# Two dense blocks and a mixture of experts on one core: in a mixed pair of expert steps, the overflow blocks' weight loads are listed before the first four's

## The reference

```python
def hierarchical_moe(h, router_group, router_expert, w_gate, w_up, w_down):
    ...
    # 4 groups of 8 experts: the best group, and in it the two best experts of each token
    combine = jnp.sum(jax.nn.one_hot(expert_id, N_EXPERTS, dtype=jnp.float32) * top_w[..., None], axis=1)
    for grp in range(N_GROUPS):
        hg = jnp.einsum("td,edf->tef", ht, w_gate[sl])      # 1024 -> 256 for each of 32 experts
        hu = jnp.einsum("td,edf->tef", ht, w_up[sl])
        act = jax.nn.silu(hg) * hu * combine[:, sl, None]
        y = y + jnp.einsum("tef,efd->td", act, w_down[sl])  # 256 -> 1024
```

## Time and profile before

| | us |
|---|---|
| median of three runs | 2850.46 |
| lowest and highest | 2848.6, 2853.78 |
| the profiled execution | 2856.73 |
| its span, first to last instruction | 2854.6 |
| granted TensorE clock, mean | 0.962 |

### The profile page before, as it was taken

The page is one execution under the profiler, slowest core; times in us unless marked ns, Lnnn a source line. Parts: engine busy times, 40 slices in busy tenths (PEclk is TensorE's granted clock), DMA queues, the critical chain, the costliest instruction groups (busy, mean ns, idle before and its releaser), DMA issues.

```text
span 2854.6 us, 35316 instructions
## 1 busy us (share of the span) xinstructions
PE 2707.4 (95%) x14474; PEld 2163.0 (76%) x14474; DVE 1534.1 (54%) x2709; ACT 968.1 (34%) x1723; POOL 57.5 (2%) x59
## 2 busy tenths in 40 slices
PE   6999999999999999999999989999999989997896
PEld 3888887876667888888888878798998787784343
DVE  3776754356224777738767444645555764444111
ACT  3322224257123322224222243634444533322111
POOL 0000000000000000000000000000000000001320
PEclk8999998999999999999999999999999899997898
DMA  7344442210222444433466423044534122256997
GB/s 300 140 191 181 184 174 75 90 41 1 88 104 98 167 184 183 179 118 148 164 256 266 154 103 111 23 167 148 187 150 167 59 85 73 80 230 254 404 368 300
DMA packets 56959, 456.54 MB, mean 160 GB/s; under 512 B 10720, under 2 KB 21344, under 8 KB 21856
## 3 DMA queue, kind: packets, MB, share of 16 engines
q1 hardware_dynamic: 49600, 446.01, 40.7%
q0 software_dynamic: 6912, 6.32, 0.7%
q10 hardware_dynamic: 288, 1.97, 0.2%
HBM read 497.25 MB, written 1.05 MB: 175 GB/s over the span
## 4 chain that ended last, share of the span: by engine, by line
PE 86%; DVE 5%; DMA 5%; ACT 3%; issue 1%; POOL 0%; SPq 0%; DVEq 0%; ACTq 0%; POOLq 0%
PE ps L497 59%; PE ps L1221 3%; PE ps L1562 2%; PE ps L2173 2%; PE ps L1213 1%; PE ps L3144 1%; DMA wr<-edn 1%; PE ps L1141 1%; PE ps L1118 1%; DMA wr<-eup 1%; DMA wr<-eup,extra_ids 1%; PE ps L502 1%; PE ps L2780 1%; PE ps L2232 1%; DMA BIG<-eup 1%
## 5 line engine op out<-in xcount | busy, mean ns | idle before, releaser
L497 PE MATMUL ps<-UL,fh 128*128 128x512 f32 (+1 forms) x1408 | 517.2, 367 | 22.5 <-DVE UL L751 21.5
L497 PE MATMUL ps<-UH,fl 128*128 128x512 f32 (+1 forms) x1408 | 515.2, 366 | 0.0
L497 PE MATMUL ps<-UH,fh 128*128 128x512 f32 (+1 forms) x1408 | 514.6, 366 | 0.0
L491 DVE TENSOR_TENSOR fl<-wr,fh 128x1024 fp32r<-128x1024 f32 (+1 forms) x304 | 328.7, 1081 | 245.5 <-ACT fh L484 245.4
L484 ACT CAST fh<-wr 128x1024 fp32r<-128x1024 f32 (+1 forms) x304 | 282.7, 934 | 199.2 <-PE ps L497 181.5
L497 PEld LDWEIGHTS ps<-UL,fh 128*128 128x128 f32 x1408 | 268.7, 191 | 68.5 <-DVE UL L751 21.3
L543 DVE SCALAR_TENSOR_TENSOR acc<-wr,CA 128x1024 f32<-128x1024 f32 x256 | 312.7, 1222 | 3.7
L497 PEld LDWEIGHTS ps<-UH,fh 128*128 128x128 f32 x1408 | 269.2, 191 | 42.1
L497 PEld LDWEIGHTS ps<-UH,fl 128*128 128x128 f32 x1408 | 269.3, 191 | 41.5
L497 PE MATMUL ps<-HH,fh 128*128 128x512 f32 (+1 forms) x704 | 255.2, 363 | 0.0
L497 PE MATMUL ps<-HL,fh 128*128 128x512 f32 (+1 forms) x704 | 255.2, 362 | 0.0
(11 more groups left out here) (501 smaller groups left out, 4178.0 us busy)
## 6 DMA issues: line engine op xcount, KB each, us to landing
wr<-ws SPq DMA_DIRECT2D x130, 2048.0 KB, 7.8
wr<-ws SPq DMA_DIRECT2D x32, 1408.0 KB, 5.9
BIG<-eup SPq DMA_DIRECT2D x30, 1024.0 KB, 19.7
wr<-eup SPq DMA_DIRECT2D x28, 1024.0 KB, 12.3
BIG<-edn SPq DMA_DIRECT2D x15, 1024.0 KB, 18.4
wr<-edn SPq DMA_DIRECT2D x14, 1024.0 KB, 15.4
wr<-ws SPq DMA_DIRECT2D x8, 1536.0 KB, 6.4
wr<-ws SPq DMA_DIRECT2D x9, 1024.0 KB, 4.8
```

What stands on the lines that cost most here:

```text
L491: e.tensor_tensor(lv, raw_tile(sp.units[n]), hv.bitcast(F32), ALU.subtract).then_inc(*low_done.inc("low", event))
L497: i = e.matmul(out, l, r, start=first and n == 0, stop=last and n == len(pairs) - 1, skip_group_check=True)
```

## The change

`expert_loads()` lists a pair's loads with its two fours the other way round whenever one of them is a beyond four. The list is used for handing out places and for the order on the two issuing queues. The order of TensorE's steps, `QUADS` and everything else stay.

```diff
@@ -214,9 +214,12 @@
 def expert_loads():
 
+
     out = []
     for g in range(FOURS // 2):
         quads = (2 * g, 2 * g + 1)
+        if "beyond" in (QUADS[p][0] for p in quads):
+            quads = quads[::-1]
         out += [("eup", n, h) for h in range(2) for p in quads for n in slots_of(p)]
         out += [("edn", n, 0) for p in quads for n in slots_of(p)]
     return out
```

## The result

Six runs of the changed kernel have a median of 2864.8 us (2858.43 to 2870.8), six runs of the kernel before beside them 2852.89 us (2848.6 to 2854.93). The ratio is 1.0039, 95% interval 1.0029 to 1.005: **slower by about 11.1 us** (8.3 to 14.3), where 6.7 had been forecast. 2864.8 lies above the range's upper end of 2861.

The account below looks back on a forecast made before the run. The prediction asked whether and when the DMA engines run dry, since the experts end when the last weights land. Its terms 5.8 + 0.4 + 0.5 = +6.7 us on 2850.46 gave 2857.2 us, range 2852.5 to 2861.

Parts of the forecast that it names:

- the last seam: Pair 4 to 5: eight loads start only at 2775.86 at the earliest, DMA engines run dry, +5.8 us (4.9 to 6.5).
- the first seam: Pair 0 to 1: beyond 0's up loads come earlier, first 2's later; forecast as +0.4 and +0.5 us.
- Rival C: Last seam: its eight loads find the DMA engines still busy, order among equal loads worth 0, 2850.5 us; chance 0.06.
- the step from the rule to "worth 0": All queues share the same 16 DMA engines, so moving loads between queues' turns is worth 0; time stays 2850.5 us.
- up a0 of pair 1: First seam: this up step starts at 2647.3 instead of 2642.44, +4.8 us, as beyond loads share the time.
- together +0.5: Pair 1's down a: real down loads 1.2 us earlier, a 2.9 us wait, 1.7 us slower step; bounds -2.5 and +2.
- The 0.4 us without work: Pair 1's down loads wait for the later up a0: moving restarts at 2655.4 against 2655.0, +0.4 us dry.
- It carries a shift of pair 1 on about one to one.: Chain from pair 1's down b through pairs 2 to 4, to the issue at 2775.86, passes on pair 1's shift.
- rival B: Pair 1's down b ends 2.5 us earlier, pair 2's up b1 stops waiting, gaps fill: +2.3 us, 2852.8; chance 0.20.
- Between two mixed pairs nothing changes: Pairs 2, 3 and 4: old and new order hand over places in the same way, so no time is added.
- X itself covers them, 0: First seam: SyncE's issue behind X is held until X moves, now holding three loads; cost 0.
- rival D: Later up a0 of pair 1 opens a gap of some 3 us, nothing returns it: +9.7 us, 2860.2; chance 0.13.

Follow-up runs that it names:

- the kernel that has this seam alone: Kernel before, with pair 5's places handed to first 7's four before first 6's, issue order kept: 2861.05 us, 1.0029.
- the first seam alone: Changed kernel with pair 5's places handed out in the other order and X's load issued third of its four: 2854.29 us, 1.0006 against the kernel before.

## Why the prediction was wrong in size

**Right: the last seam.** Predicted: no issue until up b1 of pair 4, five in a row, eup 24,0 landing 6.0 us after its issue, the end +5.8 (4.9 to 6.5). After: issued at 2778.89, landed 5.4 us later; 6.0 us dry; +6.2 in the ledger, +6.5 in the kernel that has this seam alone. Its size by itself is less sure: 8.3 us by the ratio in the order of before, 3.4 between the two kernels with the first seam and X third (1.0018 and 1.0006), where the hole is 4.1 us since up b1 of pair 4 was not slow. Rival C and the step from the rule to "worth 0" fall: 1.0029 for other places with the same order of issue, 1.0021 for another order with the same places. That the queues share one total rate is not touched by this.

**Right: up a0 of pair 1.** +5.1 against 4.8, a wait of 9.01; up a1 without its 5 us wait.

**Too small: pair 1.** The term "together +0.5" was 3.0. Its down loads did not land 1.2 us earlier (4.33 us of wait instead of the 2.9 of the sum), and the matmuls after the wait took 6.08 us, 2.4 more than 3.64, not 1.7. The 0.4 us without work ahead of it doesn't show: no window from 2604 to 2680 is under 0.96 busy.

**Wrong: "It carries a shift of pair 1 on about one to one."** +3.0 became -1.5 in pair 2, since up a1 no longer waited (1.17 before), and up b1 waited 1.50 us instead of 2.48 and no longer ran slow (3.64 instead of 5.34). This is rival B's mechanism, though not by its way (down b was not earlier). Alone, the first seam is +1.7 us and not told from 0. So the first seam is near the 0.9 that was forecast, by luck: two errors cancel.

**Wrong, and the step that made the size wrong: "Between two mixed pairs nothing changes"**, with "X itself covers them, 0". The walk through the place loop compared who waits for whom. It noted that X's load goes from third to first of its four, asked only what is held behind it at the first seam, put that at 0, and dropped it for pairs 2 to 5. The releases are indeed the same there; but the time when the 1 KB packets move is not, and the last two empty loads of pair 3 lose the stretch in which they could pass. Worth +6.0 (3.4 to 8.3) alone, 0 to 2 us by medians and ratios without the empty loads; in after it is +5.4 in pair 3 (3.9 in the second execution), and 3.5 us of dry DMA engines at 2746. Inside the changed kernel it is less sure: 4 to 6 us with the last seam in, 2.6 with it undone (1.0015 and 1.0006, on two chips; their traces end 5.7 us apart).

The three parts alone are 8.3 + 6.0 + 1.7 = 16 us, the whole 9.1 to 11.1 in its two comparisons. Each part's interval is 2.5 us wide either way, so 16 is known to some 4. Taken out of kernels that have the first seam, X's place and the last seam are both smaller (2.6 and 3.4) than alone (6.0 and 8.3), which speaks for parts that overlap, but the intervals don't rule out scatter; this stays open. So does whether rival D's picture, nothing paid back, ever holds: its 9.7 was near the result for another reason.

None of the kernels that keep all the loads beats the kernel before: the best, the first seam alone and X's load last, can't be told from it at 1.0006 and 1.0005.

## What to carry to other kernels

When a list's order changes, compare more than who releases whom: also which kinds of load move at the same moment, since the two queues here shared the DMA engines by turns and not by bytes. A load whose rows are all out of bounds was not free beside big packets; leaving the 36 out was worth 4.3 us. And where a transfer-bound stage has its next loads issued by one step of another engine, count the work queued at that moment: here a release 9 us later left the DMA engines dry for 6, as a count of loads in flight had said.

## What was new of the hardware

- Empty indirect loads took turns one to one with SyncE's packets (106 to 106 in 2 us). Beside 8 KB packets the third and the fourth landed 2.6 us apart, beside 1 KB packets 0.3; from the fourth's issue to its landing it was 9.1 to 11.4 us, and 7.7 to 7.8 where X's 1 KB packets ran in the same stretch.
- A wait can cost more than its length, and how much is not set by the length alone. Over the 13 traces every step of the experts after a wait of up to 1.87 us took 3.64 us. After 1.89 to 3.01 us some took 3.64 and some 4.9 to 5.3: 5.34 after 1.89 (last step of the kernel before with X first), but 3.64 after 2.94 (up b1 of pair 4 in the second execution of the changed kernel). The granted clock behind that wait of 2.94 was 1.00; behind the 3.01 us of the first execution (2774 to 2776) it was 0.50, the 1.2 GHz level. After 3.57 us and more every step took 5.1 to 6.6.
- At the restart from a dry stretch a load of 1 MB landed 5.4 us after its issue, close to the 5.0 of a load by itself.
